# Score tiles of the dilated attention two at a time, high and low keys side by side, and an order of its own for the last head

## The chip, the cores and the metric

One core of a Trainium2 chip runs the whole program in one launch. The metric is the device time of that core in microseconds, the median of three runs. The engines are TensorE (PE, with its weight loads PEld), VectorE (DVE), ScalarE (ACT), GpSimd (POOL) and SyncE (SP), which issues the DMAs.

## The reference

Two sequences of 512 tokens (the two batches) pass two layers and a last norm. The first layer is a mixture of three dilated window attentions with eight heads of 128; the second is a multi-head latent attention. The first layer, cut to what matters:

```
h = rms_norm(x, norm_g[0]);  proj = h @ a_w_in          # 3 groups x (q, k, v) and a gate, 8 heads x 128
for g, (window, dil) in enumerate(((128, 1), (512, 4), (2048, 16))):
    s = q_g @ k_g.T * 128**-0.5 - slope[g, h] * |t - t'|  # only |t - t'| a multiple of dil, at most 64 steps
    lse_g = logsumexp(s);  o_g = softmax(s) @ v_g
o = sum_g softmax_g(lse) * o_g
x = x + (o * silu(gate)) @ a_w_out
h = rms_norm(x, norm_g[1])                                # the second layer begins
```

Everything is float32.

## The kernel before, in words

A float32 product is made of split operands: each operand has a high part, rounded to the type in which TensorE runs at full rate (`F32R`), and a low part, the rest. A product is then three matmuls, high x high, high x low and low x high (`SPLIT_PRODUCT`, line 34), added in PSUM. ScalarE writes high parts out of PSUM, and VectorE subtracts them and writes low parts.

`stage_a` (line 147) is the first layer. It goes over the heads: heads 0, 1 and 7 are written out, 2 to 6 are a loop on every engine. A head has ten projections in the order of `PROJ` (line 38): q0, k0, v0, q1, k1, v1, gate, q2, k2, v2, each for batch 0 and then batch 1, 24 matmuls of 512 columns (`project`, line 688, matmul in line 701) into one of two banks.

The tokens are ordered so that tokens of one residue modulo 4 lie together. Group 0 has scores `s0` on its window: four of a head, two per batch, a bank each (line 772). For the dilations 4 and 16 (`s1`, `s2`) a batch's scores are four tiles of 128 queries by 128 keys, all in one bank, three matmuls of 128 columns a tile (line 780). All scores share the two banks `sum_ps`. `take_scores` (line 552) adds the bias on VectorE and writes `prob`; for s1 and s2 that is one addition of 128x512 per batch (line 572). The order is: s0 of both batches after both halves of v0, s1 of both after v1, s2 of batch 0 behind (k2, 1) and of batch 1 behind (v2, 0).

`SUMS` and `sum_no` (lines 73 to 77) number the scores of all heads; TensorE waits with `sum_taken` for a bank to be read, VectorE with `sum_done` for its scores. Maxima (`maxima`) and exponentials (`exps`) follow on VectorE and ScalarE; at a head's end `joint_softmax` (line 581) makes the weights of the groups, and POOL multiplies them onto `prob` (line 293).

The rest of head h runs during head h + 1, spread over its projections by the table `BETWEEN` (line 131): the turns of v2, four turns of the probabilities a batch (`turn`, transposes by TensorE in line 714, high parts by ScalarE, low parts by VectorE, two banks `turn_ps`), and the value products (`weigh_values`, lines 744 and 749). `GATED` says where VectorE multiplies the gate on and, with ScalarE, splits the result into `yT` (lines 625 and 627; ScalarE in line 436). The 16 output rows of the head (`output`, line 794, 3 matmuls of 512 columns each, and `add_rows`, line 613) stand beside the last four projections (`ROW_SLOTS`, line 85).

For head 7 there is no next head. TensorE, ScalarE and VectorE walk the same table without projections (lines 669 and 835), then come all 16 rows of both batches from `last_rows` (line 94), on four banks. As rows are added, ScalarE squares each of the eight row tiles of `X` (line 452). The stage ends when all engines are done.

`stage_b_in` (line 850) starts the second layer: on VectorE `rate(0)` makes the means (line 1023), POOL the power of -1/2 (line 943), and then VectorE scales the first four row tiles (`scale`, line 1032), TensorE turns them (line 1138) and ScalarE and VectorE split them (lines 963 and 1042). ScalarE first waits for four small loads (`small_loaded`).

Of the kernel before, what the change touches and what calls it, by code (L numbers as in the profile page):

```python
# [10 lines left out]
F32 = mybir.dt.float32  # L11
# [61 lines left out]
SUMS = {"s0": 0, "s1": 4, "s2": 6}  # L73


def sum_no(h, kind, n):
    return h * 8 + SUMS[kind] + n

# [15 lines left out]
def last_rows():  # L94

    return [(2 * i + half, half, i) for i in range(NT) for half in range(2)]
# [44 lines left out]
DVE_STEPS = 13  # L141
# [5 lines left out]
def stage_a(nc, io, X, next_ss, ident, minus_half, x_loaded):  # L147


    with ExitStack() as ctx:  # L150
# [7 lines left out]
        qk = [sb(f"qk{s}", [P, 2, NB, S], F32R) for s in "hl"]  # L158
# [30 lines left out]
        row_ps = sum_ps + out_ps  # L189
# [87 lines left out]
        def _(pool):  # L277
# [20 lines left out]
            with pool.Fori(1, A_HEADS) as h:  # L298
                weigh_probs(h)

        @block.scalar
        def _(act):
# [38 lines left out]
            def take(h, name, b):  # L341
# [3 lines left out]
                if name[0] in "qk":  # L345
                    g = int(name[1])

                    if g:
                        act.wait_ge(sum_done, sum_no(h, f"s{g - 1}", 3 if g == 1 else 1) + 1)
                    elif not is_first(h):  # L350
                        act.wait_ge(sum_done, h * 8)
# [74 lines left out]

            def between(h, name, b):
                for step in BETWEEN.get((name, b), ()):
                    if step[0] == "v2":
                        turn(h, "v2", step[1], lambda slot, part, g=step[1]: val[part][:, 2, g])  # L430
                    elif step[0] == "turn":
                        turn(h, "p", 4 * step[1] + step[2], lambda slot, part: pT[part][:, slot, :])
                if (name, b) in GATED:
                    yb = GATED[name, b]
                    act.wait_ge(y_ready, h * 2 - 1 + yb)
                    act.activation(yT[HI][:, yb, :], y[:, :], ACT.Copy).then_inc(y_hi, 1)
# [7 lines left out]
            for name in ("q0", "k0", "v0", "q1"):  # L444
                for b in range(NB):
                    between(A_HEADS, name, b)
            for i in range(NT):

                act.wait_ge(row_taken, row_no(A_HEADS, 2 * i + 1) + 1)
                if i >= QT:  # L450
                    act.wait_ge(row_squared, i - QT + 1)
                act.activation(scaled_x[:, i % QT, :], X[:, i, :], ACT.Square,
                               accum_out=next_ss[:, i:i + 1]).then_inc(row_squared, 1)

        @block.vector
        def _(dve):
# [61 lines left out]
            def take(h, name, b):  # L518
# [9 lines left out]
                elif name == "gate":  # L528
# [3 lines left out]
                    chain(dve.tensor_scalar(gb, gb, 1.0, None, ALU.add), h, 1 + 2 * b)  # L532
                    chain(dve.reciprocal(gb, gb), h, 2 + 2 * b)
# [18 lines left out]
            def take_scores(h, kind, n):  # L552
# [4 lines left out]
                g = int(kind[1])  # L557
                if g == 0:
                    b = n // 2
# [8 lines left out]
                else:  # L568
                    dst = prob[:, 1, n, :, (g - 1) * P:g * P]
                    src = bias[:, (5 + g) * P:(6 + g) * P].unsqueeze(1).broadcast_to((P, QT, P))  # L570
                    ps = sum_ps[slot][:].rearrange("p (t k) -> p t k", t=QT)
                dve.tensor_tensor(dst, ps, src, ALU.add).then_inc(sum_taken, 1)  # L572
                return at
# [7 lines left out]
            def joint_softmax(h):  # L581
# [6 lines left out]
                chain(ins, h, 7)  # L588
                chain(dve.tensor_tensor(joint[:], st_tile[:, :, :, 0], st_dil[:, :, :, 0], ALU.max), h, 8)
# [4 lines left out]
                chain(dve.tensor_tensor(den[:, 1], fac[:, 1], st_dil[:, :, :, 1], ALU.mult), h, 9)  # L594
                chain(dve.tensor_tensor(den[:, 0], den[:, 0], den[:, 1], ALU.add), h, 10)
                chain(dve.reciprocal(den[:, 1], den[:, 0]), h, 11)
                dve.tensor_tensor(wt[:, 0], fac[:, 0], den[:, 1], ALU.mult)
                chain(dve.tensor_tensor(wt[:, 1], fac[:, 1], den[:, 1], ALU.mult), h, 12)
# [16 lines left out]

            def between(h, name, b):
                for step in BETWEEN.get((name, b), ()):
                    if step[0] == "v2":
                        turn(h, "v2", step[1], lambda slot, part, g=step[1]: val[part][:, 2, g])
                    elif step[0] == "turn":  # L620
                        turn(h, "p", 4 * step[1] + step[2], lambda slot, part: pT[part][:, slot, :])
                if (name, b) in GATED:
                    yb = GATED[name, b]
                    dve.wait_ge(o_done, h * 2 - 1 + yb)
                    dve.tensor_tensor(y[:, :], out_ps[yb][:, :], gate[:, yb, :], ALU.mult).then_inc(y_ready, 1)
                    dve.wait_ge(y_hi, h * 2 - 1 + yb)
                    dve.tensor_tensor(yT[LO][:, yb, :], y[:, :], yT[HI][:, yb, :], ALU.subtract).then_inc(y_split, 1)
# [8 lines left out]
            def head(h):  # L636
                for name in PROJ:
                    for b in range(NB):
# [5 lines left out]
                        if (name, b) in (("k2", 1), ("v2", 0)):  # L644
                            at = take_scores(h, "s2", 1 - b)
                            maxima(h, 1, slice(1 - b, 2 - b), at, 6 - b)
                    if name == "v0":
                        for n in range(4):
                            at = take_scores(h, "s0", n)
                    if name == "v1":  # L650
                        for b in range(NB):
                            take_scores(h, "s1", b)
# [16 lines left out]
            for name in ("q0", "k0", "v0", "q1"):  # L669
                for b in range(NB):  # L670
                    between(A_HEADS, name, b)
            add_rows(A_HEADS, last_rows(), row_ps)

        @block.tensor
        def _(pe):
# [79 lines left out]
            def score(h, kind, n):  # L755
# [18 lines left out]
                else:  # L774
                    b = n
                    pe.wait_ge(proj_taken[b], proj_no(h, "k" + kind[1]) + 1)
                    for t in range(QT):
                        cols = slice(t * P, (t + 1) * P)
                        for m, (x, z) in enumerate(SPLIT_PRODUCT):
                            ins = pe.matmul(ps[:, cols], qk[x][:, 0, b, cols], qk[z][:, 1, b, cols],  # L780
                                            start=(m == 0), stop=(m == 2))
                ins.then_inc(sum_done, 1)

            def output(h, rows, banks):

                for r, half, i in rows:
                    if r == 0:
                        pe.wait_ge(out_split, h)
                        pe.wait_ge(y_split, h * 2)
# [7 lines left out]

            def between(h, name, b):

                for step in BETWEEN.get((name, b), ()):  # L800
                    if step[0] == "v2":
                        turn_values(h, 2, step[1], h - 1)
                    elif step[0] == "turn":
                        turn_probs(h, *step[1:])
                    else:
                        weigh_values(h, *step[1:])

            def head(h):
                for name in PROJ:
                    for b in range(NB):  # L810
# [7 lines left out]
                        if (name, b) in (("k2", 1), ("v2", 0)):  # L818
                            score(h, "s2", 1 - b)
                    if name == "v0":  # L820
                        for n in range(4):
                            score(h, "s0", n)
                    if name == "v1":
                        for b in range(NB):
                            score(h, "s1", b)
# [9 lines left out]
            for name in ("q0", "k0", "v0", "q1"):  # L835
                for b in range(NB):
# [1060 lines left out]
```

## Time and profile before

| | |
|---|---|
| runs | 1840.05 us, median of 3 (1839.97 to 1840.76) |
| profiled execution | 1839.34 us, its span 1837.6 us |
| granted TensorE clock, mean | 0.98 |
| first stage | until about 1197 us of the span |
| VectorE, ScalarE, POOL busy | 1085.2, 726.6, 400.3 us |

The profile shows one execution. TensorE's instructions are pipelined, so a matmul's shown duration is longer than the distance to the next one's start; what it costs in a stream is that distance. "Idle before" in brackets is the time in which the engine had nothing to run, and what ended it. In 40 slices of the span, the shares of TensorE's and VectorE's time and the granted clock are (digits are tenths):

```profile
PEld 5888888888888888888888888578686788888884
DVE  5344365355355445455445534653797898988986
PEclk9999999999999999999999999889899999999997
```

The first stage takes slices 1 to 26.

### The profile page before, as it was taken

What the parts mean: (1) busy time and instruction counts of PE and PEld (TensorE: products, weight loads), DVE (VectorE), ACT (ScalarE), POOL (GpSimd) and SP (SyncE); (2) the same over time, 40 slices, a digit from 0 to 9 for tenths busy, and PEclk for the clock granted to TensorE, in tenths of its full rate; (3) what the DMA queues carried; (4) which work ended last, traced back from release to release, by engine and by line L of the source; (5) the groups of instructions that cost most, each with busy time, mean ns of one, the idle gap of its engine ahead of it and who ended that gap; (6) DMA issues with size and microseconds to landing.
All of it is one profiled execution on the core that took longest, in us unless ns stands there. A gap on an engine that the chain in (4) does not pass through costs nothing. (4 is left out here: it accounts for less than half of the span.)

```text
span 1837.6 us, 24762 instructions
## 1 busy us (share of the span) xinstructions
PE 1748.7 (95%) x8848; PEld 1478.6 (80%) x8848; DVE 1085.2 (59%) x1878; ACT 726.6 (40%) x1465; POOL 400.3 (22%) x320
## 2 busy tenths in 40 slices
PE   6999999999999999999999999689898999999995
PEld 5888888888888888888888888578686788888884
DVE  5344365355355445455445534653797898988986
ACT  5223323313312322322322322342215877777774
POOL 1001001001001001000100100111003877777764
PEclk9999999999999999999999999889899999999997
DMA  4111111111111011111111110020100000000002
GB/s 160 47 35 69 35 35 69 35 35 58 34 46 57 34 34 57 34 37 66 34 34 57 35 58 0 1 99 1 46 24 26 27 26 26 26 26 26 6 7 109
DMA packets 23241, 76.75 MB, mean 42 GB/s; under 512 B 3088, under 2 KB 3216, under 8 KB 22928
## 3 DMA queue, kind: packets, MB, share of 16 engines
q1 hardware_dynamic: 23184, 75.98, 12.1%
q8 instruction: 37, 0.61, 0.1%
q14 instruction: 20, 0.16, 0.0%
HBM read 71.77 MB, written 4.19 MB: 41 GB/s over the span
## 5 line engine op out<-in xcount | busy, mean ns | idle before, releaser
L701 PE MATMUL bankA<-hTh,wh 128*128 128x512 f32 x1280 | 505.4, 395 | 0.4 <-DVE hTl L477 0.4
L701 PE MATMUL bankA<-hTh,wl 128*128 128x512 f32 x1280 | 499.2, 390 | 0.0
L701 PE MATMUL bankA<-hTl,wh 128*128 128x512 f32 x1280 | 498.4, 389 | 0.0
L701 PEld LDWEIGHTS bankA<-hTh,wl 128*128 128x128 f32 x1280 | 240.2, 188 | 51.6
L701 PEld LDWEIGHTS bankA<-hTh,wh 128*128 128x128 f32 x1280 | 240.4, 188 | 48.6 <-issue 1.1
L701 PEld LDWEIGHTS bankA<-hTl,wh 128*128 128x128 f32 x1280 | 240.6, 188 | 47.9
L293 POOL TENSOR_TENSOR prob<-prob,wt_blk 128x1024 f32<-128x1024 f32 x16 | 32.3, 2020 | 1074.9 <-DVE wt_blk L601 1074.9
L527 DVE TENSOR_TENSOR qkl<-bankA,qkh 128x512 fp32r<-128x512 f32 x96 | 66.4, 692 | 287.7 <-ACT qkh L355 287.4
L355 ACT ACTIVATE qkh<-bankA 128x512 fp32r<-128x512 f32 x96 | 57.3, 596 | 367.2 <-PE bankA L701 367.2
L613 DVE TENSOR_TENSOR X<-bankA,X 128x512 f32<-128x512 f32 x128 | 83.9, 685 | 52.8 <-PE bankA L794 52.8
L503 DVE TENSOR_TENSOR wl<-raw,wh 128x1024 fp32r<-128x1024 f32 x78 | 102.8, 1318 | 15.7 <-ACT wh L325 13.3
L1416 POOL TENSOR_TENSOR probb<-probb,inv 128x512 f32<-128x512 f32 x96 | 99.9, 1041 | 43.4 <-DVE inv L1607 37.5
L572 DVE TENSOR_TENSOR prob<-bankA,bias 128x512 f32<-128x512 f32 x64 | 39.8, 621 | 100.3 <-PE bankA L780 87.9
L374 ACT ACTIVATE prob<-prob,negmax 128x256 f32<-128x256 f32 x128 | 63.5, 497 | 88.0 <-DVE negmax L579 88.0
L1611 DVE TENSOR_TENSOR pTbl<-bankC,pTbh 128x512 fp32r<-128x512 f32 x128 | 87.1, 686 | 18.1 <-ACT pTbh L1521 16.6
L510 DVE TENSOR_TENSOR pTl<-bankA,pTh 128x512 fp32r<-128x512 f32 x64 | 42.8, 688 | 91.7 <-ACT pTh L339 91.6
L1510 ACT ACTIVATE probb<-bankC,negmaxb 128x512 f32<-128x512 f32 x128 | 87.6, 688 | 10.3 <-DVE negmaxb L1600 9.0
L1521 ACT ACTIVATE pTbh<-bankC 128x512 fp32r<-128x512 f32 x128 | 75.2, 595 | 32.2 <-PE bankC L1705 31.6
L1624 DVE TENSOR_TENSOR X<-bankC,X 128x512 f32<-128x512 f32 x128 | 84.8, 680 | 4.0 <-PE bankC L1740 2.8
L1600 DVE TENSOR_REDUCE negmaxb<-bankC 128x1 f32<-128x512 f32 x128 | 86.2, 680 | 1.3 <-PE bankC L1694 1.0
L325 ACT ACTIVATE wh<-raw 128x1024 fp32r<-128x1024 f32 x80 | 84.3, 1053 | 0.2 <-DMA raw<-a_w_in 0.2
L1705 PEld LDWEIGHTS bankC<-ident,probb 128*128 128x128 f32 x512 | 63.6, 141 | 19.3 <-issue 3.9
(208 smaller groups left out, 3594.5 us busy)
## 6 DMA issues: line engine op xcount, KB each, us to landing
raw<-a_w_in SPq DMA_DIRECT2D x80, 512.0 KB, 3.3
bias<-alibi SPq DMA_DIRECT2D x8, 512.0 KB, 3.3
raw_out<-a_w_out SPq DMA_DIRECT2D x8, 512.0 KB, 4.1
graw<-b_w_gate SPq DMA_DIRECT2D x8, 512.0 KB, 3.6
raw_o<-b_w_out SPq DMA_DIRECT2D x16, 256.0 KB, 2.6
raw_q<-b_w_q SPq DMA_DIRECT2D x8, 384.0 KB, 4.0
X<-x_prompt SPq DMA_DIRECT2D x4, 512.0 KB, 5.5
X<-x_sample SPq DMA_DIRECT2D x4, 512.0 KB, 8.8
```

The source lines that it names most:

```text
L325: act.activation(w[HI][:, slot, :], raw[:, slot, :], ACT.Copy).then_inc(w_hi, 1)
L503: dve.tensor_tensor(w[LO][:, slot, :], raw[:, slot, :], w[HI][:, slot, :], ALU.subtract).then_inc(w_split, 1)
L527: dve.tensor_tensor(lo, ps, hi, ALU.subtract).then_inc(proj_taken[b], 1)
L613: dve.tensor_tensor(X[:, n, cols], banks[r % len(banks)][:, :], X[:, n, cols], ALU.add).then_inc(row_taken, 1)
L701: ins = pe.matmul(proj_ps[b][:, :], w[a][:, slot, k * P:(k + 1) * P], hT[c][:, k, b * S:(b + 1) * S], start=(i == 0), stop=(i == last))
L1416: pool.tensor_tensor(tile, tile, inv[:, u, t:t + 1].to_broadcast([P, S]), ALU.mult).then_inc(prob_ready, 1)
L1510: act.activation(prob[:, u % 2, t, :], ps[:, :], ACT.Exp, bias=negmax[:, u, t:t + 1], accum_out=total[:, u, t:t + 1]).then_inc(ring_taken[ ...
L1521: act.activation(pT[HI][:, kb % 2, :], turn_ps[turning(p, s)[1]][:, :], ACT.Copy).then_inc(turn_hi, 1)
L1600: dve.tensor_reduce(negmax[:, u, t:t + 1], ps[:, :], AX.X, ALU.max, negate=True).then_inc(negmax_ready, 1)
L1611: dve.tensor_tensor(pT[LO][:, kb % 2, :], turn_ps[turning(p, s)[1]][:, :], pT[HI][:, kb % 2, :], ALU.subtract).then_inc(turn_taken, 1)
L1624: dve.tensor_tensor(X[:, i, cols], ps[:, :], X[:, i, cols], ALU.add).then_inc(ring_taken[slot], 1)
L1705: ins = pe.transpose(turn_ps[bank][:, t * P:(t + 1) * P], prob[:, u % 2, t, kb * P:(kb + 1) * P], ident[:, :])
```

## The change

Four things are done.

1. A dilated tile is two matmuls. High and low parts of queries and keys now lie in one tensor (`qk_parts`), and the first matmul multiplies the high queries with high and low keys at once (256 columns); the second adds low queries x high keys onto the first 128 columns. So a tile takes 256 columns of a bank, and a batch's four tiles take two banks in turn. A head has 12 scores to number instead of 8.
2. VectorE takes a batch's dilated scores in four additions of 128x256 (`take_dilated`): the high-key halves of two banks with the bias, a wait for its own writes, then the low-key halves onto that.
3. The scores s0 and s1 of a batch stand behind that batch's half of v0 and v1, no longer behind both halves.
4. Head 7's rest has its own order, `LAST_TURNS`: rows of batch 0 stand between turns and value products of batch 1, squares of row tiles and the mean of the first four (`rate`) stand between rows, and POOL takes the power in this stage. The rows use the banks `proj_ps + sum_ps`. The next stage starts with the scaling.

```diff
-SUMS = {"s0": 0, "s1": 4, "s2": 6}
+SUMS = {"s0": 0, "s1": 4, "s2": 8}
+SUMS_OF_HEAD = 12
...
+LAST_TURNS = [("v2", 0), ("v2", 1), ("turn", 0, 0), ("turn", 0, 1), ("weigh", 0, 0), ("turn", 0, 2), ("weigh", 0, 1),
+              ("turn", 0, 3), ("weigh", 0, 2), ("turn", 1, 0), ("weigh", 0, 3), ("gated", 0), ("turn", 1, 1),
+              ("weigh", 1, 0), ("turn", 1, 2), ("row", 0), ("row", 1), ("weigh", 1, 1), ("turn", 1, 3),
+              ("row", 2), ("row", 3), ("weigh", 1, 2), ("row", 4), ("row", 5), ("weigh", 1, 3), ("gated", 1),
+              ("square", 0), ("row", 6), ("row", 7), ("square", 1), ("square", 2), ("square", 3), ("rate", 0)]
+for i_last in range(NT // 2, NT):
+    LAST_TURNS += [("row", 2 * i_last), ("row", 2 * i_last + 1), ("square", i_last)]
...
-        qk = [sb(f"qk{s}", [P, 2, NB, S], F32R) for s in "hl"]
+        qk_parts = sb("qk", [P, 2, 2, NB, S], F32R)
+        qk = [qk_parts[:, part] for part in (HI, LO)]
...
-        row_ps = sum_ps + out_ps
+        row_ps = proj_ps + sum_ps
...
+            pool.wait_ge(mean_ready, NB + 1)
+            pool.tensor_tensor(after["rstd"][:, 0:QT], after["ms"][:, 0:QT], minus_half[:, 0:QT],
+                               ALU.pow).then_inc(rstd_ready, 1)
+            pool.wait_ge(rstd_ready, NB + 1)
...
+            for step in LAST_TURNS:                                   # ScalarE
+                if step[0] == "gated":
+                    take_gated(A_HEADS, step[1])
+                elif step[0] == "square":
+                    last_square(step[1])
+                else:
+                    stand_between(A_HEADS, step)
...
+            def take_dilated(h, kind, b, step):
+                g = int(kind[1])
+                src = bias[:, (5 + g) * P:(6 + g) * P].unsqueeze(1).broadcast_to((P, 2, P))
+                def halves(pair):
+                    ps = sum_ps[sum_slot(kind, 2 * b + pair)][:].rearrange("p (t z k) -> p t z k", t=2, z=2)
+                    return prob[:, 1, b, 2 * pair:2 * pair + 2, (g - 1) * P:g * P], ps
+                for pair in range(2):
+                    at = sum_no(h, kind, 2 * b + pair)
+                    dve.wait_ge(sum_done, at + 1)
+                    dst, ps = halves(pair)
+                    ins = dve.tensor_tensor(dst, ps[:, :, 0], src, ALU.add)
+                chain(ins, h, step)
+                for pair in range(2):
+                    dst, ps = halves(pair)
+                    dve.tensor_tensor(dst, ps[:, :, 1], dst, ALU.add).then_inc(sum_taken, 1)
+                return at
...
-                            at = take_scores(h, "s2", 1 - b)
-                            maxima(h, 1, slice(1 - b, 2 - b), at, 6 - b)
-                    if name == "v0":
-                        for n in range(4):
-                            at = take_scores(h, "s0", n)
-                    if name == "v1":
-                        for b in range(NB):
-                            take_scores(h, "s1", b)
+                            at = take_dilated(h, "s2", 1 - b, 9 - 2 * b)
+                            maxima(h, 1, slice(1 - b, 2 - b), at, 10 - 2 * b)
+                        if name == "v0":
+                            for n in (2 * b, 2 * b + 1):
+                                at = take_scores(h, "s0", n)
+                        if name == "v1":
+                            take_dilated(h, "s1", b, 1 + b)
...
+                elif step[0] == "rate":                               # VectorE, in LAST_TURNS
+                    dve.wait_ge(row_squared, QT)
+                    dve.tensor_scalar(after["ms"][:, 0:QT], after["ss"][:, 0:QT], 1.0 / D, RMS_EPS, ALU.mult,
+                                      ALU.add).then_inc(mean_ready, 1)
...
-                    for t in range(QT):
-                        cols = slice(t * P, (t + 1) * P)
-                        for m, (x, z) in enumerate(SPLIT_PRODUCT):
-                            ins = pe.matmul(ps[:, cols], qk[x][:, 0, b, cols], qk[z][:, 1, b, cols],
-                                            start=(m == 0), stop=(m == 2))
+                    for i in range(2):
+                        cols = slice((2 * pair + i) * P, (2 * pair + i + 1) * P)
+                        at = 2 * P * i
+                        pe.matmul(ps[:, at:at + 2 * P], qk[HI][:, 0, b, cols], qk_parts[:, :, 1, b, cols],
+                                  start=True, stop=True)
+                        ins = pe.matmul(ps[:, at:at + P], qk[LO][:, 0, b, cols], qk[HI][:, 1, b, cols],
+                                        start=False, stop=True, skip_group_check=True)
...
-                        pe.wait_ge(y_split, h * 2)
+                    if is_past(h):
+                        if i % QT == 0:
+                            pe.wait_ge(y_split, h * 2 - 1 + i // QT)
+                    elif r == 0:
+                        pe.wait_ge(y_split, h * 2)
...
-            rate(0)                                                   # stage_b_in, VectorE
-            dve.wait_ge(rstd_ready, 1)
             scale(0, 0)
```

TensorE's loops over `PROJ` and over the last head's steps change as VectorE's do.

## Rows read from the trace of the kernel before

**Rows 1.** The page: TensorE's busy time, share of the span, instructions.
```profile
PE 1748.7 (95%) x8848; PEld 1478.6 (80%) x8848; DVE 1085.2 (59%) x1878; ACT 726.6 (40%) x1465; POOL 400.3 (22%) x320
```
**Rows 2.** TensorE in order of time (start, duration, work): tile scores of two heads.
```profile
187.51 0.36 PE L772 MATMUL bankA<-qkh 128*128 128x256 f32 x1
...
331.00 0.36 PE L772 MATMUL bankA<-qkh 128*128 128x256 f32 x1
...
334.69 0.28 PE L772 MATMUL bankA<-qkh,qkl 128*128 128x256 f32 x1
334.81 0.38 PE L714 MATMUL bankA<-ident,vT 128*128 128x128 f32 x2
```
**Rows 3.** All engines in order of time: a group of dilated scores.
```profile
423.69 0.22 PE L780 MATMUL bankA<-qkh 128*128 128x128 f32 x1
...
423.75 0.28 PE L780 MATMUL bankA<-qkl,qkh 128*128 128x128 f32 x1
423.80 0.19 PEld L780 LDWEIGHTS bankA<-qkh,qkl 128*128 128x128 f32 x1
...
423.91 0.19 PEld L780 LDWEIGHTS bankA<-qkh 128*128 128x128 f32 x1
...
424.87 0.28 PE L780 MATMUL bankA<-qkh,qkl 128*128 128x128 f32 x1
```
**Rows 4.** TensorE in order of time: value products of 256 columns.
```profile
1174.33 0.28 PE L744 MATMUL bankA<-pTh,vall 128*128 128x256 f32 x1
...
1174.69 0.28 PE L744 MATMUL bankA<-pTh,vall 128*128 128x256 f32 x1
```
**Rows 5.** Who waited for whom: us in total, times, longest.
```profile
PE bankA L772 <- DVE prob L572: 4.1, 7, 0.6
```
**Rows 6.** VectorE's groups by line and shape: busy, mean ns, idle before.
```profile
L572 DVE TENSOR_TENSOR prob<-bankA,bias 128x512 f32<-128x512 f32 x48 | 33.1, 690 | 100.3 <-PE bankA L780 87.9 <-PE bankA L772 11.5
...
L572 DVE TENSOR_TENSOR prob<-bankA,bias 128x256 f32<-128x256 f32 x16 | 6.6, 415 | 0.0
```
**Rows 7.** VectorE in order of time: additions of rows behind k2 and v2.
```profile
423.21 1.37 DVE L613 TENSOR_TENSOR X<-bankA,X 128x512 f32<-128x512 f32 x2 [2.89 <-PE bankA L794]
...
431.41 1.37 DVE L613 TENSOR_TENSOR X<-bankA,X 128x512 f32<-128x512 f32 x2 [4.08 <-PE bankA L794]
```
**Rows 8.** TensorE in order of time: the rest of the last head.
```profile
1162.40 1.97 PE L714 MATMUL bankA<-ident,prob 128*128 128x128 f32 x8 [11.96 <-POOL prob L293]
...
1173.99 0.39 PE L744 MATMUL bankA<-pTh,valh 128*128 128x256 f32 x1 [0.98 <-DVE pTl L510]
...
1177.17 0.33 PE L749 MATMUL bankA<-pTh,valh 128*128 128x128 f32 x1 [0.61 <-DVE pTl L510]
...
1182.33 0.77 PE L794 MATMUL bankA<-w_outh,yTh 128*128 128x512 f32 x1 [2.26 <-DVE yTl L627]
...
1190.14 0.39 PE L794 MATMUL bankA<-w_outh,yTh 128*128 128x512 f32 x1
...
1194.67 0.39 PE L794 MATMUL bankA<-w_outh,yTl 128*128 128x512 f32 x1
```
**Rows 9.** Busy time of each engine in ten microseconds of that stretch, granted clock.
```profile
1180.00:1190.00 10.00, 7.74 (x28) 6.23 (x28) 6.55 (x10) 3.91 (x7) 0.00 (x0) 0.83 0.01 2
```
**Rows 10.** VectorE in order of time: the last rows, the next stage's start.
```profile
1186.22 9.57 DVE L613 TENSOR_TENSOR X<-bankA,X 128x512 f32<-128x512 f32 x14 [0.26 <-PE bankA L794]
1197.27 0.17 DVE L1023 TENSOR_SCALAR msb<-row_ss 128x4 f32<-128x4 f32 x1 [1.48 <-PEq L150]
1198.56 3.26 DVE L1032 TENSOR_SCALAR gateT<-X,rstdb 128x512 f32<-128x512 f32 x8 [1.12 <-POOL rstdb L943]
```
**Rows 11.** ScalarE in order of time: the last square, the next stage's first copies.
```profile
1195.82 1.06 ACT L452 ACTIVATE prob<-X 128x1024 f32<-128x1024 f32 x1 [0.21 <-DVE X L613]
1196.78 0.19 ACT L452 ACTIVATION_READ_ACCUMULATOR prob<-X 128x1 f32 x1
1201.51 1.48 ACT L963 ACTIVATE hTbh<-bankB,gb_col 128x512 fp32r<-128x512 f32 x2 [4.54 <-PE bankB L1138]
```
**Rows 12.** SyncE's queue in order of time: issue of the last small load.
```profile
1198.55 0.43 SPq L924 DMA_DIRECT2D rope_tab<-rope_tok  x1
```
**Rows 13.** DMA issues: count, KB, median us to landing.
```profile
rope_tab<-rope_tok SPq DMA_DIRECT2D x1, 64.0 KB, 2.0
```

More of the change, by code:

```diff
@@ L443, in _, with last_square @@
             split_out(A_HEADS)
-            for name in ("q0", "k0", "v0", "q1"):
-                for b in range(NB):
-                    between(A_HEADS, name, b)
-            for i in range(NT):
+            def last_square(i):
                 act.wait_ge(row_taken, row_no(A_HEADS, 2 * i + 1) + 1)
+                if i == 0:
+                    act.wait_ge(turned, turn_no(A_HEADS, "p", 7) + 1)
                 if i >= QT:
@@ L531, in take @@
                     gb = gate[:, b, :]
-                    chain(dve.tensor_scalar(gb, gb, 1.0, None, ALU.add), h, 1 + 2 * b)
-                    chain(dve.reciprocal(gb, gb), h, 2 + 2 * b)
+                    chain(dve.tensor_scalar(gb, gb, 1.0, None, ALU.add), h, 3 + 2 * b)
+                    chain(dve.reciprocal(gb, gb), h, 4 + 2 * b)
                     dve.tensor_tensor(gb, ps, gb, ALU.mult).then_inc(proj_taken[b], 1)
@@ L556, in take_scores @@
                 dve.wait_ge(sum_done, at + 1)
[L557 to L559 removed]
+                b = n // 2
+                if kind == "s0":
                     rows = prob[:, 0, b]
@@ L614, in add_rows, with stand_between, take_gated @@
                                       ALU.add).then_inc(row_taken, 1)
+            def stand_between(h, step):
+                if step[0] == "v2":
+                    turn(h, "v2", step[1], lambda slot, part, g=step[1]: val[part][:, 2, g])
+                elif step[0] == "turn":
+                    turn(h, "p", 4 * step[1] + step[2], lambda slot, part: pT[part][:, slot, :])
+            def take_gated(h, yb):
+                dve.wait_ge(o_done, h * 2 - 1 + yb)
+                dve.tensor_tensor(y[:, :], out_ps[yb][:, :], gate[:, yb, :], ALU.mult).then_inc(y_ready, 1)
+                dve.wait_ge(y_hi, h * 2 - 1 + yb)
+                dve.tensor_tensor(yT[LO][:, yb, :], y[:, :], yT[HI][:, yb, :], ALU.subtract).then_inc(y_split, 1)
             def between(h, name, b):
                 for step in BETWEEN.get((name, b), ()):
[L618 to L621, printed above, removed]
+                    stand_between(h, step)
                 if (name, b) in GATED:
[L623 to L627, printed above, removed]
+                    take_gated(h, GATED[name, b])
             def next_split(h, name):
@@ L668, in _ @@
             split_out(A_HEADS)
[L669 to L672, printed above, removed]
+            for step in LAST_TURNS:
+                if step[0] == "gated":
+                    take_gated(A_HEADS, step[1])
+                elif step[0] == "row":
+                    add_rows(A_HEADS, [last_row(step[1])], row_ps)
+                elif step[0] == "rate":
+                    dve.wait_ge(row_squared, QT)
+                    dve.tensor_scalar(after["ms"][:, 0:QT], after["ss"][:, 0:QT], 1.0 / D, RMS_EPS, ALU.mult,
+                                      ALU.add).then_inc(mean_ready, 1)
+                else:
+                    stand_between(A_HEADS, step)
         @block.tensor
@@ L818, in head @@
                         if (name, b) in (("k2", 1), ("v2", 0)):
[L819 to L825, printed above, removed]
+                            for pair in range(2):
+                                score(h, "s2", 2 * (1 - b) + pair)
+                        if name in ("v0", "v1"):
+                            for n in (2 * b, 2 * b + 1):
+                                score(h, {"v0": "s0", "v1": "s1"}[name], n)
                     if name in ("v0", "v1"):
@@ L834, in _ @@
             head(A_HEADS - 1)
-            for name in ("q0", "k0", "v0", "q1"):
-                for b in range(NB):
-                    between(A_HEADS, name, b)
-            output(A_HEADS, last_rows(), row_ps)
+            for step in LAST_TURNS:
+                if step[0] == "row":
+                    output(A_HEADS, [last_row(step[1])], row_ps)
+                else:
+                    stand_between(A_HEADS, step)
 B_HEADS = 16
```

85 lines of the change are left out of this document (42 added, 43 removed).

## The prediction

> **What bounds the kernel now.** I read the page's busy shares first, then TensorE's instructions in order of time, then who waited for whom, and last the 60 us in which the dilated stage ends and the next one starts. TensorE is busy for 95% of the span [rows 1], but that figure covers a stage in which it hardly ever stops and a tail in which it stops often, so each stretch needs its own limit.
>
> In the middle of the first stage a head takes 331.00 - 187.51 = 143.49 us from one first tile score to the next [rows 2]. Counting TensorE's work of a head by the spacing of starts: 480 projection and 48 row products of 512 columns at 0.227 (119.9 us; 20 of them start in 1194.67 - 1190.14 = 4.53, [rows 8]), 48 dilated scores, 48 dilated value products and 56 transposes of 128 columns at about 0.11 (16.8), 24 tile scores and 24 tile value products of 256 columns at 0.12 (5.8): 142.4 us. Only about one microsecond of a head is not TensorE's own pace. So in this stage a product that is dropped is time gained, and work on another engine costs nothing until TensorE has to wait for it.
>
> **The dilated scores.** Before, a tile is three products of 128 columns. From the second start of a group to the twelfth it is 424.87 - 423.75 = 1.12 us, 0.112 for each, and the weight loads are 423.91 - 423.80 = 0.11 apart too [rows 3]. Products of 256 columns, each with its own load, start 1174.69 - 1174.33 = 0.36 apart for three, 0.12 each [rows 4]. Twice the columns cost 0.01 more, so what a 128-column product costs is its load, not its columns. (512 columns cost 0.227, which is the columns.) After, a tile is one product of 256 columns (high queries against high and low keys) and one of 128 (low queries against high keys): 0.119 + 0.112 = 0.231 against 0.336, so 0.105 less. There are 4 tiles x 2 batches x 2 dilations x 8 heads = 128: 128 x 0.105 = 13.4 us. Bounds: two loads at 0.11 cannot pass in less than 0.22, which gives 14.8; if the wide product, reading two places of SBUF, costs as much as two narrow ones, the gain is 0. I take 13.4, because the tile scores of line 772 read keys in four pieces and still come every 0.12 (334.81 - 334.69, [rows 2]).
>
> The Trainium skill ("TensorE: Matmul & The Clock Gate", Back-to-back issue gap) states sustained spacings with weight loads of about 81 ns at 128 columns and 131 ns at 512. By these the three products would be 243 ns and the two about 98 + 81 = 179 ns, an estimate by that page, and 128 tiles would give 8.2 us. The rows above show 112 and 227 ns instead, so the sum goes by the rows.
>
> **The order of the scores.** The four tile scores of a head stood in one run behind both value projections, on two banks; the third and fourth have to wait until VectorE has taken the first and second. The run takes 334.81 - 331.00 = 3.81 us [rows 2] where 24 x 0.12 = 2.88 would do: 0.93 lost, in seven heads (3.80 to 3.81 each), and 0.43 in the first head, 6.9 us in all. The view of waits shows 4.1 of it as waiting for VectorE [rows 5]; the rest is the first loads after the wait. After, two scores follow each projection, so 24 products of 0.227 (5.45 us) lie between the second and the third, and VectorE needs 0.69 and about 1.3 us for two. The wait goes: 6.9 us. Bounds: 0, if it is only moved, and 6.9; a loss would need waits that are longer at a distance of 5.45 us than at none. The turns of the values, next in line, need the turning banks of the probabilities' last two turns; these are taken ahead of the scores on VectorE, so nothing is late next.
>
> The dilated scores split over two banks have the same kind of wait, one group to the next, but 5.45 us apart at the least.
>
> **VectorE's extra work.** One addition of 128x512 (0.69 us, [rows 6]) becomes four of 128x256, 0.415 each by the second row, with a wait of the engine for itself in the middle: 1.66 us plus that wait, against 0.69. The wait has no row here; it is more than nothing and should be less than one more addition, and I take 0.1. That is 1.0 to 1.4 us more (1.1), 32 times, 35 us of VectorE time in a stage where it idles more than half. What it delays: behind the second group (k2, v2) stand the maxima, the next weights' low part and the next rows' additions, for which TensorE's row products wait. VectorE then sits idle 2.89 us in one place and 4.08 us in the next before those rows come [rows 7], and both are longer than 1.4. So I cost it at nothing. If this cover were gone, each microsecond would stand 4 times in a head.
>
> ScalarE's waits for scores, renumbered, wait for the same events. Buffers are the same size. No DMA is added.
>
> **The last head.** Nothing in the change touches the 12 us in which TensorE waits for the weighted probabilities of the last head (its first row in [rows 8]). From there on:
>
> Before: turns and value products last from 1162.40 to about 1179.9, with waits of 0.98 and 0.61; then the gated output of the second batch goes over VectorE, ScalarE and VectorE (2.26 idle), then 16 rows to 1194.9 [rows 8]. The granted clock of the ten microseconds around that idle time is 0.83 [rows 9]: a third of them ran at the lower level (1.2 of 2.4 GHz). VectorE adds rows at 9.57 / 14 = 0.684, the last is taken at about 1195.8, ScalarE's last square follows (1.16 with its read), and VectorE starts the next stage at 1197.27; its first scaling starts at 1198.56, because mean and power take 1.29 [rows 10, 11].
>
> After: a turn of the second batch moves ahead of the first batch's last value product, which still ends at about 1172. Row 0 must wait for that batch's gated output, by the same chain 2.4 us after that end: 1174.5. A turn, a value product and another turn fill 1.6 of this, 0.8 stays idle. From there TensorE goes on without a wait: six rows (6 x 0.68 = 4.1), value products of 0.72, 1.34 and 1.34 (6 x 0.12, 12 x 0.112) and a turn of 0.44, which ends at 1182.4, 2.5 us later than before. Rows 6 and 7 fill part of the gate's wait; row 8 starts at about 1184.8. Now VectorE holds at the mean ("rate") until ScalarE has squared four rows, which it starts only after the gate's copy: from 1183.9, 4 x 1.16, so VectorE is free at about 1188.8. Behind that wait stand the additions of rows 8 to 15: TensorE fills its four banks by 1187.5 and then idles 2 us. Eight additions at 0.684 end at 1194.3, against 1195.8: 1.5 gained. The mean and power are now behind that wait instead of between the stages: 1.29 gained. But the small vectors of the next stage then arrive late: the last is issued 1.3 us into the stage and takes 2.0 [rows 12, 13], so ScalarE's first turn starts at about 3.35 and not 2.95: 0.4 back. That makes 2.4 us. If TensorE's clock falls in the 2 us of idling, as it did after 2.26 us before, the last four rows cost 1.28 each and 1.5 of it is lost. I take 2.0 (bounds 0.9 and 2.8).
>
> **Sum.** 13.4 + 6.9 + 2.0 = 22.3 us. The profiled execution took 1839.34 (span 1837.6, 1.7 around it): 1817.0. The median of the three runs, 1840.05, is 0.7 above the profiled one, so I forecast 1817.8 and add the 0.7 to the times of the rivals too.
>
> **Rivals.**
> 1. *The wait of the tile scores stays.* For: two banks and the same takers. Against: 5.45 us of products in between. Only 13.4 + 2.0 is gained: 1824.6.
> 2. *A wide product costs its columns twice.* For: no row shows a wide product followed by a narrow one in a steady stream. Against: line 772. Then 6.9 + 2.0: 1831.1.
> 3. *A dropped narrow product frees less than its spacing*, because loads run ahead of the products. For: the second of a group starts 0.06 after the first, behind 512 columns (423.75 - 423.69, [rows 3]). Against: the ten that follow don't. At 0.06 less the 0.007 by which the wide one is longer, 128 tiles give 6.8 and the time is 1824.4. The page's figures above point the same way: 1822.9 by their estimate.
> 4. *Slower: VectorE becomes the bound in the stretch of k2 and v2.* The additions stand ahead of the rows' additions, and TensorE's rows 12 to 15 wait for those. It decides as soon as the extra time is more than the 2.89 us idle there; I take 1.1. To end slower than before it must cost 22.3 / 8 = 2.8 us a head. If the whole of the additions (1.2 with the hand-over, 4 a head, 8 heads) were exposed, 38 us come on top: 1817.8 + 38 = 1856.
> 5. *More is gained:* half-clock stretches after the stage fall otherwise and the tail gives its full 2.8; 1813 or somewhat less.
>
> **How the numbers follow.** The forecast, 1813.5 to 1821 by its own bounds, has 0.74; rival 1 0.08, rival 2 0.05, rival 3 0.04, rival 4 0.04, rival 5 0.05. Range 1813 to 1825: it takes in rivals 1 and 3 and leaves out 2 and 4. A measurement of this kernel tells about 0.2% (3.7 us) from no change. Faster 0.93, within 0.2% 0.02, slower 0.05.
>
> **What would show it.** Right: the lines of the dilated scores hold 128 products of 256 and 128 of 128 columns instead of 384, and a tile's starts span 0.23; TensorE's waits for the tile scores' additions are gone; a head takes 143.5 - 16 x 0.105 - 0.93 = 140.9 us; the stage's first scaling comes some 2.4 us sooner than the heads alone explain. VectorE's wait at the mean is visible as 3 us of idling with TensorE idle behind it. Wrong: a head above 141.9 (a new wait of TensorE, by its name in the view of waits), or a wide product at 0.22.

## The result

The changed kernel takes **1815.78 us** (median of 4 runs, 1815.0 to 1816.51); the kernel before, run beside it, 1840.4 (4 runs). The ratio is 0.9867, 95% interval 0.9855 to 0.988: 24.6 us or 1.3% faster. The forecast was 1817.8 in a range of 1813 to 1825. The profiled execution took 1816.16 us with a span of 1814.4, so 23.2 less than the profiled one of before, where the sum said 22.3.

The page's line of engines, which answers to [rows 1]: 128 products fewer, 18.8 us less of TensorE, 22.3 us more of VectorE.

```profile
PE 1729.9 (95%) x8720; PEld 1462.7 (81%) x8720; DVE 1107.5 (61%) x1974; ACT 726.2 (40%) x1465; POOL 400.8 (22%) x320
```

TensorE in order of time (start, duration, work): first the later pair of tile scores in two heads, then a group of dilated scores, for [rows 2, 3].

```profile
187.79 1.67 PE L825 MATMUL bankA<-qk 128*128 128x256 f32 x12
...
328.59 1.67 PE L825 MATMUL bankA<-qk 128*128 128x256 f32 x12
...
1121.64 0.28 PE L833 MATMUL bankA<-qk 128*128 128x256 f32 x1
1121.75 0.22 PE L835 MATMUL bankA<-qk 128*128 128x128 f32 x1
1121.81 0.34 PE L833 MATMUL bankA<-qk 128*128 128x256 f32 x1
1121.98 0.22 PE L835 MATMUL bankA<-qk 128*128 128x128 f32 x1
1122.04 0.34 PE L833 MATMUL bankA<-qk 128*128 128x256 f32 x1
...
1122.45 0.22 PE L835 MATMUL bankA<-qk 128*128 128x128 f32 x1
1122.51 0.45 PE L754 MATMUL bankA<-hTh,wh 128*128 128x512 f32 x1
```

A head takes 328.59 - 187.79 = 140.80 us instead of 143.49. Eight products do a group of four tiles in 1122.51 - 1121.64 = 0.87 us; before, twelve took 1.29 (a group from 1141.19 to the next projection product at 1142.48). That is 0.42 a group, and there are 32: 13.4. Within the group a narrow product starts 0.17 behind its wide one (1121.81 to 1121.98) and the next wide one 0.06 behind that, 0.23 together; the first tile takes less, 0.17.

VectorE's groups (busy, mean ns, idle before), then one taking (the additions of one batch's dilated scores) in order of time with the row additions behind k2 and v2, for [rows 6, 7].

```profile
L610 DVE TENSOR_TENSOR prob<-bankA,bias 128x256 f32<-128x256 f32 x64 | 25.6, 420 | 64.0 <-PE bankA L835 63.3
L614 DVE TENSOR_TENSOR prob<-bankA,prob 128x256 f32<-128x256 f32 x64 | 24.2, 420 | 1.1
...
411.20 0.75 DVE L610 TENSOR_TENSOR prob<-bankA,bias 128x256 f32<-128x256 f32 x2
411.98 0.76 DVE L614 TENSOR_TENSOR prob<-bankA,prob 128x256 f32<-128x256 f32 x2
...
417.19 1.37 DVE L655 TENSOR_TENSOR X<-bankA,X 128x512 f32<-128x512 f32 x2 [1.81 <-PE bankA L853]
...
424.93 1.37 DVE L655 TENSOR_TENSOR X<-bankA,X 128x512 f32<-128x512 f32 x2 [3.46 <-PE bankA L853]
```

A taking lasts 411.20 to 412.74, 1.54 us against 0.69. The idle time ahead of the rows shrank from 2.89 to 1.81 and from 4.08 to 3.46, and is not used up.

The end of the stage, for [rows 8 to 11]: TensorE's rows, VectorE with the mean (L722) and the next stage's first scaling (L1093), ScalarE's last square and the next stage's first copy (L1024), and ten microseconds with the granted clock (third figure from the right).

```profile
1127.79 0.39 PE L754 MATMUL bankA<-hTh,wl 128*128 128x512 f32 x1
...
1165.80 0.50 PE L853 MATMUL bankA<-w_outh,yTh 128*128 128x512 f32 x1 [0.75 <-DVE yTl L668]
...
1170.03 0.50 PE L853 MATMUL bankA<-w_outh,yTh 128*128 128x512 f32 x1 [1.22 <-DVE X L655]
...
1172.69 0.40 PE L853 MATMUL bankA<-w_outh,yTl 128*128 128x512 f32 x1
...
1177.38 5.85 PE L1197 MATMUL bankB<-ident,gateT 128*128 128x128 f32 x32 [4.29 <-DVE gateT L1093]
```

```profile
1169.21 0.17 DVE L722 TENSOR_SCALAR row_ms<-row_ss 128x4 f32<-128x4 f32 x1 [2.27 <-ACT prob L471]
1169.29 4.87 DVE L655 TENSOR_TENSOR X<-bankA,X 128x512 f32<-128x512 f32 x8
1175.65 3.26 DVE L1093 TENSOR_SCALAR gateT<-X,row_rstd 128x512 f32<-128x512 f32 x8 [1.49 <-PEq L160]
...
1175.16 0.19 ACT L471 ACTIVATION_READ_ACCUMULATOR prob<-X 128x1 f32 x1
1178.92 2.42 ACT L1024 ACTIVATE hTbh<-bankB,gb_col 128x512 fp32r<-128x512 f32 x4 [3.58 <-DMA rope_tab<-rope_tok]
...
1168.00:1178.00 10.00, 4.49 (x21) 3.15 (x20) 7.30 (x15) 5.78 (x12) 1.01 (x1) 1.00 0.02 1
```

The last projection product starts 20.0 us sooner than before (1147.80 to 1127.79), the first scaling 22.9, ScalarE's first copy 22.6, and the execution ends 23.2 sooner. VectorE's 2.27 of idling at the mean, and TensorE's 1.22 behind it, are new.

### The profile page after: what moved, and what is told of

It is laid out like the page before. It is cut to its first block and busy times, and to the rows that moved or that the text cites. A ratio compares the mean times of both kernels' runs of the same rounds, so it can differ in the third digit from the quotient of the medians.

```text
span 1814.4 us, 24638 instructions
## 1 busy us (share of the span) xinstructions
PE 1729.9 (95%) x8720; PEld 1462.7 (81%) x8720; DVE 1107.5 (61%) x1974; ACT 726.2 (40%) x1465; POOL 400.8 (22%) x320
## 5 line engine op out<-in xcount | busy, mean ns | idle before, releaser
L554 DVE TENSOR_TENSOR qk<-bankA,qk 128x512 fp32r<-128x512 f32 x96 | 66.4, 692 | 287.1 <-ACT qk L370 286.9
L370 ACT ACTIVATE qk<-bankA 128x512 fp32r<-128x512 f32 x96 | 57.2, 596 | 366.8 <-PE bankA L754 366.8
L1670 DVE TENSOR_TENSOR pTbl<-bankC,pTbh 128x512 fp32r<-128x512 f32 x128 | 87.1, 685 | 17.9 <-ACT pTbh L1580 16.3
L1569 ACT ACTIVATE probb<-bankC,negmaxb 128x512 f32<-128x512 f32 x128 | 87.5, 688 | 10.2 <-DVE negmaxb L1659 9.0
L1764 PE MATMUL bankC<-ident,probb 128*128 128x128 f32 x512 | 75.9, 274 | 2.3 <-ACT probb L1576 2.1
```

Of the source, the lines that this page charges most:

```text
L1569: act.activation(prob[:, u % 2, t, :], ps[:, :], ACT.Exp, bias=negmax[:, u, t:t + 1], accum_out=total[:, u, t:t + 1]).then_inc(ring_taken[ ...
L1670: dve.tensor_tensor(pT[LO][:, kb % 2, :], turn_ps[turning(p, s)[1]][:, :], pT[HI][:, kb % 2, :], ALU.subtract).then_inc(turn_taken, 1)
L1764: ins = pe.transpose(turn_ps[bank][:, t * P:(t + 1) * P], prob[:, u % 2, t, kb * P:(kb + 1) * P], ident[:, :])
```

## The experiments

All edits are to the changed kernel and are shown in outline; `...` marks what is left out. Times are medians. "More" is against the 1815.78 us of the changed kernel unless another number is given; run again beside other variants it took 1814.31, so such a difference carries some 1.5 us. Where a run's tail is compared, the measure is the distance from the last projection product to the next stage's first product of TensorE (L1197): 52.49 us in the kernel before, 49.59 in the changed one (1177.38 - 1127.79), since the head ahead of it moves by up to a microsecond from profile to profile. The tail itself moves too: in the six profiles that have the changed order of the last head and no work added to VectorE, it is 48.6 to 49.6.

**Tile scores in one run again**

```
-  score(s0, two of batch b)        # behind v0 of batch b
+  score(s0, all four)              # behind both batches of v0
```

> The changed kernel with the four tile scores of a head again in one run behind both halves of v0; the rest stays. Theory (the run's third and fourth score wait for VectorE's additions, 0.9 us a head): TensorE waits at the third tile score in every head, a head's period goes from 140.79 back to about 141.6 (the run was 3.81 long before and is 1.52 + 1.51 now, 0.78), 5.5 to 6.9 us more in all: about 1822. Rival (the wait is only moved, another wait takes its place in the changed kernel): within 1 us of 1815.8.

1821.29 us (1820.5 to 1822.42), 5.5 more; head 141.66. TensorE's second pair of tile scores, then its row in the view of waits (total, times, longest):

```profile
327.42 1.67 PE L825 MATMUL bankA<-qk 128*128 128x256 f32 x12
329.67 1.71 PE L825 MATMUL bankA<-qk 128*128 128x256 f32 x12 [0.58 <-DVE prob L594]
...
PE bankA L825 <- DVE prob L594: 4.1, 7, 0.6
```

The wait of [rows 5] is back with its own 4.1 us, and 0.87 a head with it.

**The same for the scores of v1** (both groups behind both batches of v1)

> The changed kernel with the scores of dilation 4 of both batches behind both halves of v1, as they stood before the change. Theory (two banks, and now two banks a batch: the second batch's first score waits until VectorE has added both halves of the first batch's): about 1.1 us of waiting a head at the third score, 8 heads, 9 us more: about 1825, with a row TensorE waits for VectorE's second additions. Rival (the new place of these scores has no part in the result): within 1 us of 1815.8.

1824.11 us (1823.65 to 1824.44), 8.3 more; head 142.00. In this order the wait is 7.8 us in 8 places:

```profile
PE bankA L834 <- DVE prob L614: 7.8, 8, 1.0
```

A tile now takes twice the bank, so a batch's four tiles fill both banks, and in the changed kernel it is the distance between the two batches' groups that keeps TensorE from waiting for them.

**The wide product as two narrow ones**

```
-  pe.matmul(ps[high|low], q_high, k_high|k_low)
+  pe.matmul(ps[high], q_high, k_high)
+  pe.matmul(ps[low],  q_high, k_low)
```

> The changed kernel, but the wide product of a dilated tile is two narrow ones again (high x high and high x low, in the same columns of the bank as now); VectorE's four additions stay. Theory (a narrow product costs its weight load, about 0.11): a group of four tiles takes 1.29 instead of 0.87, 32 groups, 13.3 us more: about 1829. Rival 1 (the saving is not in the products): within 1 us. Rival 2 (a dropped narrow product frees 0.05 only): 6.8 more, 1822.6.

1829.46 us (1828.2 to 1829.86), 13.7 more; head 142.63, 1.84 more. This is the value of the wide product alone, with VectorE's four additions kept. The two parts, 1.84 and 0.87, make 2.71, which is all that a head gained (143.50 to 140.79).

**The second product 256 columns wide too** (low queries against high and low keys, which adds the product of the low parts)

> The changed kernel, but the second product of a dilated tile covers 256 columns too (low queries against high and low keys; the term low x low is added, which the kernel leaves out). 128 columns more in each of 128 tiles. Theory (the load is what a narrow product costs, columns are hidden behind it): 0.12 instead of 0.11 for the second product, at most 0.02 a tile, 1 to 2.6 us more in all. Rival (columns cost their streaming time, 0.053 for 128): 6.8 us more, 1822.6.

1815.65 us (1814.75 to 1816.28), no difference; head 141.00, 0.21 more, and in its profile the tail and the later stages gave back what the heads lost, which is no more than they differ by from profile to profile. 128 columns more cost about 0.013 us a product (0.21 / 16): from 128 to 256 columns, it is not the columns that pace these products. That the pace is the weight load's was read from the loads, 0.11 apart; as every product here has a load of its own, no run parts the load from a fixed price of a product.

**More work for VectorE** (a reciprocal that nobody uses, in each of a head's four takings): 128x512, 3.34 us each

> The changed kernel with one reciprocal of 128x512 (3.35 us, into a tile that nobody reads) in the middle of each of VectorE's four takings of dilated scores in a head: three times the time that the change added there. Theory (VectorE's queue has room: the first takings of a pair may be 4.4 us late for s1 and 5.3 us for s2 before TensorE's next group waits, the head's end 4.2 us before the first turn of the next head waits): no more than 1.5 us, about 1816. Rival (VectorE is the bound as soon as the extra time is over the 1.8 us in which it idles before the rows behind k2): 1.5 us a head at the least, 1828 or more, up to 107 us if all of it is exposed.

1845.61 us (1843.37 to 1846.23), 30 more. My expectation fell. TensorE's waits, and where the first stands:

```profile
PE bankA L757 <- DVE qk L555: 12.3, 7, 3.2
PE bankA L856 <- DVE w_outl L652: 11.7, 7, 1.7
...
529.12 0.50 PE L856 MATMUL bankA<-w_outh,yTh 128*128 128x512 f32 x1 [1.68 <-DVE w_outl L652]
```

A head grew by 3.78: 1.97 at the row product that needs the output weights' low part, which VectorE makes behind v1's second taking, and 1.81 at k0 of the next head, which needs the bank of q0; VectorE frees that only after the joint softmax behind v2's. Then 128x896 (5.9 us each):

> The same with a reciprocal of 128x896, about 5.9 us, which is more than the room that I read. Theory: TensorE now waits in each head, about 1.5 us at the second group of s1, 0.6 at the second group of s2, and some 3 us at the first turn of the probabilities of the next head, because the head's joint softmax starts about 7 us late: 5 us a head, 35 to 40 us in all, about 1853. Rival (there is room for this too): within 2 us of 1816.

1942.44 us, 127 more; the same two waits grew to 28.4 us each, others joined them, and the mean granted clock fell to 0.962 from 0.981. A head grew by 16.3, and about 3.9 of it are products at half pace behind the two long waits (starts 0.43 apart instead of 0.23). And 128x256 (1.74 us each):

> In each of a head's four dilated takings one reciprocal of 128x256, about 1.7 us, half of the 3.35 us of the run with one of 128x512; it computes nothing that is used. Theory (read from that run's trace): a pair of takings has about 4.9 us of room on VectorE before TensorE waits (6.7 us were added there, and TensorE stood 1.7 to 1.8 us behind each pair), so a pair's 3.4 us cost nothing: head period 140.8 to 141.2 us, time 1815 to 1819 us. Rival: VectorE's added work costs in proportion (3.78 us a head for 13.4 us), then 1.9 us a head: period 142.7, time about 1830 us.

1817.07 us (1816.93 to 1818.08), 2.8 more than the 1814.31 of the changed kernel beside it; head 141.16 to 141.21. The 0.37 that a head lost stands at the row product alone. So the room behind v1's second taking, which is how late VectorE may be there before TensorE loses time, is 1.74 - 0.37 = 1.37 us, and the run with 128x512 says the same: 3.34 - 1.97 = 1.37. (The first taking's addition hides in the wait for the second group.) Behind k2 and v2, 3.5 us for the two cost nothing.

**All sixteen rows behind both gates, the mean behind the last**

> The changed kernel with all 16 rows of the last head again behind both batches' gated outputs, and the mean behind the last row (the power still in this stage, off the path). Theory (of the 2.6 us that the tail gained, about 0.9 are the mean and the power, and 1.6 the rows between the turns): 1.6 us more, 1817.4. Rival 1 (the rows between the turns gain nothing, because VectorE waits at the mean afterwards): within 0.5 us of 1815.8. Rival 2 (they are all of it): 2.6 more.

1812.0 us (1809.9 to 1812.84), where I and the rivals expected a loss or no change. The tail is 47.87, 1.7 shorter.

**Squares 0 to 2 ahead of the second gate's copy, the mean behind row 9**

> A version meant to be better: squares 0 to 2 of the last head stand on ScalarE ahead of the second gate's copy, where it idled 5.5 us, and VectorE takes the mean behind row 9 instead of ahead of row 8. Theory (VectorE idled 2.27 us at the mean, with eight additions queued behind it; then the last rows come at TensorE's pace of 0.68): the stage ends 1.9 us sooner, about 1813.9, and VectorE's wait at the mean is gone. Rival (something else ends the stage, or the later gate costs as much): within 0.5 us of 1815.8.

1812.07 us (1810.96 to 1812.53); tail 47.24. The kernel before took 1838.65 beside these two, not 1840.4, so the changed kernel, this one and a third order were run side by side:

> The changed kernel once more, unedited, beside the two tail orders of this call. Theory: the two earlier tail variants (rows last 1812.0 us, squares early 1812.1 us) are really about 2 to 4 us faster than the changed kernel, so this run gives 1814.5 to 1816.5 us. Rival: what they gained was the day's runs (the kernel before stood 1 to 2 us lower beside them), and this run gives 1812 to 1813.5 us too.

1814.31 us (1814.11 to 1815.44); tail 49.41.

> The kernel with squares 0 to 2 ahead of the second gate's copy and the mean behind row 9, once more, beside the changed kernel. Theory: VectorE no longer stands 2.27 us at the mean, so the end of the stage is 2 to 2.4 us sooner and the time 2 to 4 us below the changed kernel of this call (1811 to 1813.5 us against 1814.5 to 1816.5). Rival: no difference beyond 0.7 us.

1810.62 us (1809.93 to 1811.46); tail 47.26. VectorE's last step of the second batch's gated output (L669), then the mean and what stands behind it:

```profile
1163.93 0.69 DVE L669 TENSOR_TENSOR yTl<-y,yTh 128x512 fp32r<-128x512 f32 x1 [0.70 <-ACT yTh L451]
...
1167.04 0.17 DVE L723 TENSOR_SCALAR row_ms<-row_ss 128x4 f32<-128x4 f32 x1
1167.12 4.02 DVE L656 TENSOR_TENSOR X<-bankA,X 128x512 f32<-128x512 f32 x6
1172.63 3.26 DVE L1094 TENSOR_SCALAR gateT<-X,row_rstd 128x512 f32<-128x512 f32 x8 [1.49 <-PEq L161]
```

The idle 2.27 is gone. The third order has the last head as before, with the new early power:

```
-  ..., row 0, row 1, weigh, turn, row 2, row 3, weigh, row 4, row 5, weigh, gated 1, ...
+  ..., weigh, turn, weigh, weigh, gated 1, then rows 0 to 15, a square behind every second one, mean
```

> The last head's values turned and weighed in the order that the kernel before had, then both gates, then all 16 rows with the mean behind the last; the power stays with GpSimd at the end of the stage. Theory (from rows last): rows put between turns hold back the second gate by what they take, and a mean that waits for the fourth square with eight rows behind it holds the rows 2.27 us; with neither, the end of the stage is about where rows last had it, and the time within 1.5 us of it, 1811 to 1814 us, 2 to 4 us below the changed kernel beside it. Rival 1: the new order of the turns (batch 1's first turn ahead of batch 0's last weighing) is worth about a microsecond, so 1814 to 1816 us. Rival 2: the tail's order as a whole is what the prediction took it for, 2.0 us in favour of the changed kernel: 1817.5 us or more.

1810.98 us (1810.07 to 1812.96); tail 48.08. TensorE's first row, then VectorE:

```profile
1159.53 0.45 PE L853 MATMUL bankA<-w_outh,yTh 128*128 128x512 f32 x1
...
1161.12 0.69 DVE L668 TENSOR_TENSOR yTl<-y,yTh 128x512 fp32r<-128x512 f32 x1 [0.70 <-ACT yTh L450]
1161.73 9.96 DVE L655 TENSOR_TENSOR X<-bankA,X 128x512 f32<-128x512 f32 x16
1171.61 0.16 DVE L722 TENSOR_SCALAR row_ms<-row_ss 128x4 f32<-128x4 f32 x1
1173.36 3.26 DVE L1093 TENSOR_SCALAR gateT<-X,row_rstd 128x512 f32<-128x512 f32 x8 [1.59 <-PEq L160]
```

The order between turns is not worth the microsecond of rival 1, and rival 2 falls too: without it the kernel is 3.3 us faster. Here TensorE starts the rows with no wait, where it stood 2.26 in [rows 8], because row 0 now needs only the first batch's gated output; VectorE then adds all 16 without a break. The steps of the tail, in us behind the last projection product:

| | second gated output done | last addition done | next stage's first scaling | its first product on TensorE |
|---|---|---|---|---|
| kernel before | 34.38 | 47.98 | 50.76 | 52.49 |
| changed kernel (beside the next two) | 37.78 | 46.20 | 47.68 | 49.41 |
| squares early | 37.53 | 44.04 | 45.53 | 47.26 |
| third order, rows last | 34.81 | 44.68 | 46.35 | 48.08 |

Against the kernel before, the third order ends its additions 3.3 sooner, by the earlier first row, and needs 1.1 less from there to the scaling, by the mean and the power inside the stage. No run undoes these one by one, or the rows' other banks, so this split is read from rows and not shown by an edit. Rows between the turns hold the second gated output back by some 3 us. But with the squares early they stand at the same places, and the additions end 0.4 to 0.6 sooner than in the two orders with all rows last (44.47 in the first of them). So what the changed order loses, 2.2 us at the last addition, is VectorE's stop at the mean, and not the rows between the turns.

Squares early (twice) and the two orders with the rows last are all faster than the changed kernel: side by side with it by 3.7 and 3.3 us, with no overlap of the runs. Between them no difference in time is shown. In the profiles of that set the tail is 2.2 and 1.3 us shorter, and the two stages behind it take 1.5 and 0.7 less. The largest part of this lies in one stretch, where TensorE works off the same products in 18.0 us in the changed kernel and in 17.0 and 16.7 in the others. The changed kernel, then the third order (the granted clock is the third figure from the right):

```profile
1221.00:1239.00 18.00, 14.23 (x80) 13.71 (x79) 8.66 (x19) 7.50 (x18) 1.08 (x2) 0.81 0.01 1
1219.00:1237.00 18.00, 14.22 (x88) 13.71 (x87) 9.20 (x19) 7.51 (x18) 1.09 (x3) 0.91 0.01 1
```

The clock is 0.91 in that stretch in the kernel before and in the variant with three narrow products too, which has the changed order of the tail. So about a microsecond of the gain is the clock's, and it is not shown that the order brings it; the tail's part is the order's.

## Why the prediction was right

- **Dilated scores: right, and in size.** 13.4 by the trace (0.42 in each of 32 groups), 13.7 by undoing it. The reading that carried it was that loads 0.11 apart set the pace of 128 columns, while 256 cost 0.01 more [rows 3, 4]. Rivals 2 (columns cost twice) and 3 (a dropped product frees less) fall with it.
- **Order of the tile scores: right.** 6.9 forecast; 0.87 a head by undoing it instead of 0.93, 5.5 us in the timed run. Nothing was late next, as said: rival 1 falls. What the prediction passed over in one sentence, that the dilated scores need the same distance, was worth more than this: 8.3 us, had the groups of v1 stood together.
- **VectorE's extra work: right in cost, incomplete in its reason.** A taking takes VectorE 0.85 longer, below the 1.0 to 1.4 expected, so 32 of them make 27 us where 35 were forecast, and TensorE loses nothing by it. But the cover read from [rows 7], 2.89 and 4.08 us, was not the narrowest. That is behind v1's second taking, at the output weights' low part, with 1.4 us left. So rival 4's point of decision (2.89) was put too high and at the wrong place; at this change's 0.85 it didn't matter. The expectation of my first run with added work repeated this step, and the 30 us of that run refuted it: the idle time ahead of one waiting instruction is the room of that instruction, not of everything behind it.
- **The tail: right in its parts, undersized by choice.** Shifted by the 20.0 us of the heads, the prediction had VectorE free of the mean at 1168.8 (trace 1169.29), the last addition's end at 1174.3 (1174.16), and the small load holding ScalarE's first copy, which the trace names: it comes 2.6 sooner than the heads explain, where the steps made 2.4. That the last addition came out so near is in part luck: the mean was 0.5 later than said, and the eight additions behind it, queued, came 0.60 apart instead of 0.684. I took 2.0 for fear of a falling clock; the granted clock is 1.00 through the stretch, and TensorE idled 1.22 there instead of 2. What the prediction did not ask is whether this order is better than its parts: it saw the stop at the mean and priced it inside the sum, but did not see that an order without the stop ends the tail some 2 us sooner.
- **The sum.** Heads 20.0 (20.3 forecast), tail 2.9 at the first scaling (2.0), the later stages 0.3. One term lost something by chance: the first head gained 1.07 instead of 2.1. TensorE's first projection products in order of time, the kernel before:

```profile
18.42 0.47 PE L701 MATMUL bankA<-hTh,wh 128*128 128x512 f32 x1
18.73 0.40 PE L701 MATMUL bankA<-hTl,wh 128*128 128x512 f32 x1
18.97 0.39 PE L701 MATMUL bankA<-hTh,wl 128*128 128x512 f32 x1
```

The changed kernel:

```profile
18.44 0.78 PE L754 MATMUL bankA<-hTh,wh 128*128 128x512 f32 x1
19.01 0.63 PE L754 MATMUL bankA<-hTl,wh 128*128 128x512 f32 x1
19.44 0.63 PE L754 MATMUL bankA<-hTh,wl 128*128 128x512 f32 x1
```

They start 0.43 apart where 0.24 is usual, so TensorE ran at about half its pace. By 21.46 us the changed kernel has got where the kernel before was at 20.33, which makes up for the missing microsecond. The clock's record has its first rise at 20.8 us here and at 18.3 before. In the variants above, whose start is the same, that rise lies anywhere between 18.0 and 20.9, so the change is not its cause.

## What to carry to other kernels

Where TensorE never waits, price a product by the spacing of its starts: where a product of 256 columns starts no later behind the last than one of 128, as here within some 0.01 us, columns are nearly free and products are not, so widen the moving side and drop products (512 columns cost 0.227). When an order brings several things at once (an earlier first row, an early mean, rows between turns), undo each alone: here the place of the mean took back some 2 us of what the others gave, and the times of the two orders with all rows last would by themselves have put it down to the rows between the turns. And read the room of an engine at every instruction that another engine waits for behind the new work, the last of a pair first.

## What the runs showed that was not expected

- A tile of two products, 256 and 128 columns, takes 0.218 us on the mean of a group (0.87 / 4), less than the 0.231 of the prediction. The pace is not the reason: from the second tile on it is 0.23. The first tile of a group is cheaper, 0.17 here, and 0.28 against 0.335 with three products before, so what a tile saves came out all the same, 0.104 (0.42 / 4) against 0.105.
- VectorE's wait for itself between the two pairs of additions is hardly visible: four additions take 1.54 us, less than 4 x 0.42, since neighbours overlap.
- Work added to VectorE past its room cost more than itself in one step, and only by the clock: from 3.34 to 5.9 us a taking, 10.2 us more a head cost 12.5. The waits make 8.6 of this; the other 3.9 are TensorE's products at half pace, as its granted clock falls in each head.
